# Branch projections released token tile by token tile, with the linear attention's norm ahead of the branch products

## What is computed

```python
z = rms_norm(x, ln_mix) @ w_in
o_nsa = nsa_attention(...)            # branch 0
o_gla = gated_linear_attention(...)   # branch 1: rms_norm(o, norm_g) * silu(r) at its end
o_mem = memory_attention(...)         # branch 2
gates = sigmoid(merge + b_merge)
merged = (gates[:, :, 0] * (o_nsa @ w_branch[0])
          + gates[:, :, 1] * (o_gla @ w_branch[1])
          + gates[:, :, 2] * (o_mem @ w_branch[2]))
x = x + merged @ w_out
```

## Time and profile before

| | us |
|---|---|
| median of 3 runs | 1996.36 |
| lowest, highest | 1995.1, 1997.03 |
| the profiled execution | 1997.19 |
| its span in the trace | 1995.5 |
| PE busy | 1960.1 (98%) |
| POOL busy | 1593.1 (80%) |
| ACT busy | 1045.1 (52%) |
| DVE busy | 750.8 (38%) |

### The profile page before, as it was taken

How to read it: one execution, slowest core, us unless ns; L and a number is a source line. 1 busy time by engine, 2 the same in 40 slices (tenths; PEclk the granted TensorE clock), 3 DMA queues, 4 the chain that set the end, 5 groups by cost and what they waited for, 6 DMA issues and landing times.

```text
span 1995.5 us, 26511 instructions
## 1 busy us (share of the span) xinstructions
PE 1960.1 (98%) x9698; PEld 1583.3 (79%) x9698; DVE 750.8 (38%) x1652; ACT 1045.1 (52%) x1748; POOL 1593.1 (80%) x1160
## 2 busy tenths in 40 slices
PE   9999999999999999999999999899999999999999
PEld 7888777888888877788887777788888777778887
DVE  4534444000300444400055688521115478742111
ACT  6445666444644566644475444654446554555443
POOL 7888876988788887698879577888888867788886
PEclk9999999999999999999999999999999999999999
DMA  6655434555665543456564333456547333345553
GB/s 234 232 206 179 159 117 157 186 186 188 211 218 190 174 157 125 166 196 240 190 253 148 117 116 127 138 182 222 208 169 274 127 127 117 119 136 195 184 186 131
DMA packets 98204, 348.63 MB, mean 175 GB/s; under 512 B 13436, under 2 KB 14108, under 8 KB 97820
## 3 DMA queue, kind: packets, MB, share of 16 engines
q1 hardware_dynamic: 97372, 345.80, 50.2%
q10 hardware_dynamic: 704, 1.14, 0.2%
HBM read 345.85 MB, written 1.05 MB: 174 GB/s over the span
## 4 chain that ended last, share of the span: by engine, by line
PE 93%; DVE 3%; POOL 2%; issue 1%; ACT 1%; DMA 0%; SPq 0%; DVEq 0%; ACTq 0%; POOLq 0%
PE psum L569 28%; PE psum L571 27%; PE psum L570 27%; PE psum L707 2%; POOL lo L542 2%; PE psum L750 1%; PE psum L637 1%; PE psum L760 1%; PE psum L982 1%; PE psum L773 1%; PE psum L740 1%; DVE big L2142 0%; PE psum L1136 0%; PE psum L837 0%; PE psum L796 0%
## 5 line engine op out<-in xcount | busy, mean ns | idle before, releaser
L542 POOL TENSOR_TENSOR lo<-raw,hi 128x256 fp32r<-128x256 f32 (+1 forms) x1156 | 1592.9, 1401 | 388.2 <-ACT hi L1270 359.6
L1270 ACT ACTIVATE hi<-raw 128x1024 fp32r<-128x1024 f32 x616 | 647.8, 1059 | 507.3 <-PE psum L571 482.8
L569 PE MATMUL psum<-hi,h_hi 128*128 128x512 f32 x1632 | 654.0, 401 | 2.3 <-POOL lo L542 2.1
L571 PE MATMUL psum<-hi,h_lo 128*128 128x512 f32 x1632 | 640.6, 393 | 0.0
L570 PE MATMUL psum<-lo,h_hi 128*128 128x512 f32 x1632 | 639.4, 392 | 0.0
L569 PEld LDWEIGHTS psum<-hi,h_hi 128*128 128x128 f32 x1632 | 308.7, 189 | 72.9 <-POOL lo L542 6.0
L571 PEld LDWEIGHTS psum<-hi,h_lo 128*128 128x128 f32 x1632 | 308.0, 189 | 66.2
L570 PEld LDWEIGHTS psum<-lo,h_hi 128*128 128x128 f32 x1632 | 308.6, 189 | 60.3
L1811 DVE SCALAR_TENSOR_TENSOR big<-psum,small,big 128x256 f32<-128x256 f32 (+1 forms) x120 | 61.1, 551 | 749.5 <-ACT big L1363 749.5
L569 PE MATMUL psum<-hi,y_hi 128*128 128x512 f32 x832 | 334.3, 402 | 8.4 <-DVE big L2262 4.9
L571 PE MATMUL psum<-hi,y_lo 128*128 128x512 f32 x832 | 325.5, 391 | 0.0
(11 more groups left out here) (265 smaller groups left out, 1396.1 us busy)
## 6 DMA issues: line engine op xcount, KB each, us to landing
raw<-in_stream SPq DMA_DIRECT2D x616, 512.0 KB, 3.3
big<-in_w SPq DMA_DIRECT2D x14, 512.0 KB, 6.9
big<-in_post SPq DMA_DIRECT2D x6, 512.0 KB, 5.3
special<-in_b_merge SPq DMA_DIRECT2D x2, 1536.0 KB, 8.1
memkv<-in_mem SPq DMA_DIRECT2D x2, 1024.0 KB, 5.7
big<-in_band SPq DMA_DIRECT2D x2, 768.0 KB, 4.8
x<-in_x SPq DMA_DIRECT2D x2, 512.0 KB, 5.0
special<-in_special SPq DMA_DIRECT2D x2, 512.0 KB, 4.4
```

Of the source, the lines that this page charges most:

```text
L542: t = pool.tensor_tensor(M.lo[:, slot, w], M.raw[:, slot, w], f32(M.hi[:, slot_hi, w]), ALU.subtract)
L569: pe.matmul(out, lhs_hi, rhs_hi, start=start, stop=False)
L571: return pe.matmul(out, lhs_lo, rhs_hi, start=False, stop=stop)
L1270: act.activation(M.hi[:, slot_hi, :], M.raw[:, slot, :], ACT.Copy).then_inc(sem["hi"], 1)
```

## The change

Three things. The tiles' banks are now given as a pair, and for branches 2 and 0 tile 0 goes to banks 2, 3 and tile 1 to 0, 1. PE waits before each tile for that tile's banks alone, and tells DVE by a new semaphore `rows` when tile 0 of a branch's last piece is done. And the steps of the linear attention's norm stand earlier: `gla` 3 to 5 behind pieces 61 and 62 (before: 62 to 64), 6 and 7 behind 64 and 65 (before: 65 and 66), with the table load of Ln and Exp right behind the last gate.

```diff
-ROWS2 = {2: 0, 0: 0, 1: 4}
+ROWS2 = {2: (2, 0), 0: (2, 0), 1: (4, 6)}
...
-        ("rows", 2): ([nu[17], gu[1][4]], [nu[18]], [gla[3]], [gla[4]]),
-        ("rows", 0): ([gla[5]], [gla[6]], [gla[7]], none),
+        ("rows", 2): ([nu[17], gu[1][4]], [nu[18], gla[3]], [gla[4], gla[5]], none),
+        ("rows", 0): ([gla[6]], [gla[7]], none, none),
...
-            t = product(psum[:, bank + 2 * m + i, :], a_hi[:, kt, m * P:m * P + P], a_lo[:, kt, m * P:m * P + P],
+            t = product(psum[:, banks[m] + i, :], a_hi[:, kt, m * P:m * P + P], a_lo[:, kt, m * P:m * P + P],
...
-    def rows(c, kt, a_hi, a_lo, bank, start, stop=False, second=None):
+    def rows(c, kt, a_hi, a_lo, banks, start, stop=False, second=lambda: None):
 
         pe.wait_ge(sem["lo"], c + 1)
         for m in range(MT):
-            if m and second:
-                pe.wait_ge(sem[second[0]], second[1])
-            t = rows_tile(c, m, kt, a_hi, a_lo, bank, start, stop)
+            if m:
+                second()
+            t = rows_tile(c, m, kt, a_hi, a_lo, banks, start, stop)
+            if stop and m == 0:
+                t.then_inc(sem["rows"], 1)
         t.then_inc(sem["used"], 1)
...
+                second = lambda: None
                 if b == 2 and i == 0:
-                    evicted(len(names) + 1)
                     evicted(len(names))
+                    second = lambda: evicted(len(names) + 1)
                 if b == 0 and i == 0:
-                    pe.wait_ge(sem["branch"], 4 * layer + 2)
+                    pe.wait_ge(sem["branch"], 4 * layer + 1)
+                    second = lambda: pe.wait_ge(sem["branch"], 4 * layer + 2)
...
                     act.activation(w, w, ACT.Sigmoid).then_inc(sem["sigmoid"], 1)
-            elif what == "branch":
-                if step[1:] == (2, 0):
+                if b == 1:
                     exp_and_ln()
...
-                dve.wait_ge(sem["used"], piece["rows", b, 3] + 1)
+                if m:
+                    dve.wait_ge(sem["used"], piece["rows", b, 3] + 1)
+                else:
+                    dve.wait_ge(sem["rows"], nxt("rows"))
```

More of the change, by code:

```diff
@@ L214 @@
 SEMAPHORES = (
-    "hi", "lo", "used", "quarter",
+    "hi", "lo", "used", "rows", "quarter",
     "x_in0", "x_in1", "ident", "const", "rot", "pre1", "pre2", "par", "mem_in", "masks", "angles", "stored", "w1_0", "w1_1",
@@ L585, in strip_piece, with rows_tile @@
         t.then_inc(sem["used"], 1)
-    def rows_tile(c, m, kt, a_hi, a_lo, bank, start, stop):
+    def rows_tile(c, m, kt, a_hi, a_lo, banks, start, stop):
         slot, slot_hi = c % RING, c % RING_HI
@@ L591, in rows_tile, with half_rows @@
             w = slice(i * 512, i * 512 + 512)
-            t = product(psum[:, bank + 2 * m + i, :], a_hi[:, kt, m * P:m * P + P], a_lo[:, kt, m * P:m * P + P],
+            t = product(psum[:, banks[m] + i, :], a_hi[:, kt, m * P:m * P + P], a_lo[:, kt, m * P:m * P + P],
                         hi[:, slot_hi, w], lo[:, slot, w], start, stop)
         return t
-    def rows(c, kt, a_hi, a_lo, bank, start, stop=False, second=None):
+    def rows(c, kt, a_hi, a_lo, banks, start, stop=False, second=lambda: None):
         pe.wait_ge(sem["lo"], c + 1)
         for m in range(MT):
-            if m and second:
-                pe.wait_ge(sem[second[0]], second[1])
-            t = rows_tile(c, m, kt, a_hi, a_lo, bank, start, stop)
+            if m:
[3 more added lines that the diff above has]
+                t.then_inc(sem["rows"], 1)
         t.then_inc(sem["used"], 1)
-    def half_rows(c, m, kt, a_hi, a_lo, bank, stop):
+    def half_rows(c, m, kt, a_hi, a_lo, banks, stop):
         if m == 0:
             pe.wait_ge(sem["lo"], c + 1)
-        t = rows_tile(c, m, kt, a_hi, a_lo, bank, False, stop)
+        t = rows_tile(c, m, kt, a_hi, a_lo, banks, False, stop)
         if m:
@@ L613, in half_rows, with last_rows @@
             t.then_inc(sem["f"], 1)
-    def last_rows(c, kts, a_hi, a_lo, bank, turn, ylo={}):
+    def last_rows(c, kts, a_hi, a_lo, banks, turn, ylo={}):
         for m in range(MT):
@@ L622, in last_rows @@
                     pe.wait_ge(sem["ylo"], ylo[i])
-                half_rows(c + i, m, kt, a_hi, a_lo, bank, i == len(kts) - 1)
+                half_rows(c + i, m, kt, a_hi, a_lo, banks, i == len(kts) - 1)
     def turned_tile(src, m, pairs, banks, ready, until):
@@ L713, in down @@
             for i in range(kts):
-                rows(c + i, (s - n0) % 2 * kts + i, y_hi, y_lo, 4, s == n0 and i == 0)
+                rows(c + i, (s - n0) % 2 * kts + i, y_hi, y_lo, (4, 6), s == n0 and i == 0)
         c += 4
@@ L730, in feed_forward @@
         order = [(strips - s) % 2 * kts + i for s in ((2, 1) if gated else (1,)) for i in range(kts)]
-        last_rows(c, order, y_hi, y_lo, 4, turn_next, {kts: n0 + strips} if gated else {})
+        last_rows(c, order, y_hi, y_lo, (4, 6), turn_next, {kts: n0 + strips} if gated else {})
         return c + 4
@@ L903, in mix1 @@
                 pe.wait_ge(sem["y1lo"], 7 * layer + Y1_EVENT[kt])
-                rows(c0 + 24 + i, kt, y_hi, y_lo, 0, i == 0, second=("z5", layer + 1) if i == 0 else None)
+                rows(c0 + 24 + i, kt, y_hi, y_lo, (0, 2), i == 0, second=lambda: pe.wait_ge(sem["z5"], layer + 1))
             elif what == "half":
@@ L908, in mix1 @@
                 pe.wait_ge(sem["y1lo"], 7 * layer + Y1_EVENT[kt])
-                half_rows(c0 + 24 + KD - 4 + i, m, kt, y_hi, y_lo, 0, i == 3)
+                half_rows(c0 + 24 + KD - 4 + i, m, kt, y_hi, y_lo, (0, 2), i == 3)
             elif what == "turn":
@@ L1202, in mix2 @@
                 pe.wait_ge(sem["y2lo"], 10 * layer + Y2_EVENT[kt])
-                rows(piece[step], kt, y_hi, y_lo, ROWS2[b], i == 0, i == 3)
+                rows(piece[step], kt, y_hi, y_lo, ROWS2[b], i == 0, i == 3, second)
             elif what == "last_branch":
@@ L1211, in mix2 @@
                 enter(V.merged, (0, 1, 2, 3), "merged", 4 * layer, c,
-                      lambda cc, m, j: rows_tile(cc, m, j, h_hi, h_lo, 4, j == 0, False), lambda j: j // 2)
+                      lambda cc, m, j: rows_tile(cc, m, j, h_hi, h_lo, (4, 6), j == 0, False), lambda j: j // 2)
                 pe.wait_ge(sem["xlo"], 8 * n["feats"])
-                last_rows(c + 4, range(4, KD), h_hi, h_lo, 4, turn_next)
+                last_rows(c + 4, range(4, KD), h_hi, h_lo, (4, 6), turn_next)
                 c += KD
@@ L2260, in branch @@
             dve.wait_ge(sem["sigmoid"], 6 * layer + 2 * (2, 0, 1).index(b) + m + 1)
-            bank = ROWS2[b] + 2 * m
+            bank = ROWS2[b][m]
             t = dve.tensor_tensor(g, g, flat(psum[:, bank:bank + 2, :]), ALU.mult)
```

## The result

| | before | changed |
|---|---|---|
| median, us | 1996.36 (7 runs) | 2000.45 (7 runs) |
| lowest, highest, us | 1992.92, 1998.26 | 1999.59, 2003.58 |
| span of the profiled execution, us | 1995.5 | 2001.0 |
| its mean granted clock | 0.994 | 0.992 |

The ratio is 1.0026, 95% interval 1.0017 to 1.0035: about 5 us more (3.4 to 7.0), and the medians differ by 4.1 us.

A forecast was written before the change was run, and what follows sets the result against it. PE was taken as the bound (93% of the chain that ended last). +2.49 us in the first layer and +1.97 in the second, +4.46 on the median 1996.36, gave 2000.8 us; range 1997.5 to 2004.0.

The forecast's parts named there:

- Part 1: PE's wait ahead of piece 60: tile 0 runs before the SiLU ends, so piece 63 ends 1.37 us earlier.
- Part 2: PE's wait ahead of piece 64: the norm delays DVE's product, so PE resumes at 1269.63, 1.97 us later than before.
- Part 3: Clock behind the stop at piece 64: falls in both layers, 1.27 us more in the first, nothing new in the second.
- longer low clock: Rival: clock low for longer behind that stop and DVE loses the race with POOL; 2004.5 us, chance 0.16.
- Part 4: What comes behind, to w_out's fourth piece: PE resumes 5.21 us after w_out's start; +2.49 us first layer, +1.97 second.
- The clock spares the kernel: Rival: the clock stays at 1.00 behind the stop at piece 64 in both layers; 1998.3 us, chance 0.18.
- The release by tiles does nothing: Rival: tile 0 of piece 60 is still held, piece 63 ends at 1265.21; time as forecast, within its 0.55.
- Not slower: Rival: the norm is ready in time and both stops go, POOL giving most back; 1994.4 us, chance 0.11.

The follow-up runs named there:

- e1: The changed kernel with the norm's steps and table load put back where they stood, release by tiles kept: 1992.22 us, ratio 0.9983 to the kernel before.
- e3: The changed kernel with the norm's guess and second multiply behind branch 2's products, its transposes behind pieces 65 and 66: 1994.34 us, ratio 0.9992 to before.
- e2: The kernel before with only the norm's steps and the table load moved forward, no release by tiles: 2007.1 us, ratio 1.0053.
- e5: The changed kernel with 20 matmuls nobody reads added on PE ahead of the wait before piece 64: 1998.51 us, ratio 1.0009 to before.
- e6: The changed kernel with squares and norm behind piece 67's rounding, both transposes behind piece 66, the second waiting for its own bank only: 1991.75 us, ratio 0.9976 to before.
- e9: e6 with the squares and the rest of the norm behind the rounding of piece 68 too: 1992.43 us, ratio 0.9975 to before.
- e7: e3 with POOL subtracting pieces 66 to 75 of the second mixer in one instruction each instead of four: 2004.86 us, ratio 1.0043 to before.

## Why the prediction was right

The forecast was 2000.8 us and the measured median 2000.45, with the ratio at 1.0026. Point by point:

**Part 1** held: 0.38 us of stop inside piece 60 where 0.3 was said, and the end of piece 63 moved as worked out.

**Part 2** held to 0.13 us. Exp ends at 1267.39 - 0.96 = 1266.43 (said: 1266.40), the four steps take 0.2 us each, the multiply is the short one (1.23), and PE resumes at 1269.76 (said: 1269.63). That the multiply came ahead of POOL was close, by 0.10 us where 0.3 was worked out. e1 and e3 show that it is the norm's place ahead of the products that makes the stop, since it goes in e1, and shrinks to 0.63 us in e3, when that is put back; e2 shows that the move does harm by itself.

**Part 3**, the clock, was right in kind and too small in size. The sum took 1.27 us in each layer with a fall, the price of the one row at hand. Measured from piece 64 to `w_out`: 26.34 us in the first layer (1297.06 - 1270.72), against 24.54 before, and e5, without a fall, 1.93 us less at the fourth piece. So the term was 1.8 to 1.9 us in the first layer and not 1.27. The stretch of half clock had begun while PE still stood and reached 4.1 us into its work. In the second layer it reached 2.9 us, and there the term held: 25.78 us against 25.81 before, which had its own fall. The first layer's 1.8 to 1.9 us lie in the range that the prediction gave the term (up to 2.54), part of the way to the rival of the longer low clock.

**Part 4**, what is given back to POOL, held in kind. The resumption at the fourth piece came 5.60 us after the start of `w_out` in both layers (said: 5.21). POOL took no longer over piece 75: from its start on it to PE's resumption there are 3.76 us (1298.90 to 1302.66), and in the row of 5.21 there were 3.77 (1785.67 to 1789.44). What came later was ACT's rounding of the piece, 0.68 us behind the start of `w_out` instead of 0.28:

```profile
1296.62 0.66 PE L639 MATMUL psum<-consts,big 128*128 128x128 f32 x4 [0.42 <-DVE big L2275]
```

```profile
1297.74 2.03 ACT L1274 ACTIVATE hi<-raw 128x1024 fp32r<-128x1024 f32 x2
```

```profile
1785.67 6.07 POOL L542 TENSOR_TENSOR lo<-raw,hi 128x256 fp32r<-128x256 f32 x5 [0.35 <-ACT hi L1270]
```

```profile
1298.90 6.05 POOL L542 TENSOR_TENSOR lo<-raw,hi 128x256 fp32r<-128x256 f32 x5 [0.34 <-ACT hi L1274]
```

The first of the two POOL lines is of the kernel before, second layer; the others are of the changed kernel. ACT rounds behind its casts of the turned `merged`, and PE had stood 0.42 us for DVE's addition to `merged` in the middle of the turning, in both layers; in the row used there was no such stop.

The sum by terms, first layer: 3.54 (said 2.49: +0.13 wait, +0.53 clock and +0.39 here). Second layer: 2.47 (said 1.97: +0.14 wait, -0.03 clock and +0.39 here). The sum for the profiled execution was thus short by 1.5 us. It stood at 2002.66, 2.2 us above the median of its kernel, so that the median nevertheless is 0.35 us from the forecast owes something to luck: in its sum the errors add up to more than in its result.

**The rivals.** "The clock spares the kernel" fell, as it did not spare it in either layer of the profiled execution; some of the other runs may have been spared in part. Four of the seven stand at 1999.6 to 2000.5 us with a mean clock of 0.994 or 0.995, the median among them, and three at 2002.4 to 2003.6 with 0.992, the profiled one among them. None of the four has a trace, so how much of the clock term is in the median is open; e5, which keeps PE busy in that stop, comes out some 3 us lower by the ratios, so the timed runs seem to pay for the clock too, but the two intervals just touch. "Longer low clock" was met halfway in the first layer, without the lost race on DVE. "The release by tiles does nothing" fell with the 0.38 us inside piece 60: tile 0 had run, and piece 63 ended 1.37 us earlier. "Not slower" fell with the date of Exp. Its number for a kernel without the stops was 1994.4; e1 came to 1992.2 and e3 to 1994.3, so the idea behind it, that POOL gives most back, was sound.

**A version that beats both** is e6 (or e1 and e9, which aren't told apart from it): 0.24% below the kernel before, and by the two ratios 0.5% below the changed one. In the changed place itself the traces show 2.5 us for e6 and 5.3 for e9.

## What to carry to other kernels

When work is moved forward in an engine's fixed order, ask what it waits for, and then everything that now stands behind it waits for the same thing: here two products of 1.2 us, which PE needed, stood behind a norm that hung on ACT's Ln and Exp, at the end of 17 us of other work on ACT. A release by finer parts is worth its freed waits only up to the next bound, and that bound may be an engine that is not the busiest over the whole span (POOL 80%, PE 98%): the date at which ACT's roundings, 52% busy, let POOL begin set the time 30 us later. A stop of PE can cost more than its length, since PE may resume at half the clock (here 1.9 us more, by e5).

## What the runs showed of the hardware

Small DVE instructions beside POOL were dearer than I had allowed. The norm's four small steps took 0.17 to 0.18 us each with POOL idle (changed kernel), 0.56 to 0.67 beside POOL's quarters (e6), and three of them 2.1 to 2.3 beside POOL's whole pieces (e7), where each ended with the POOL instruction under way.

```profile
1266.66 0.56 DVE L1720 TENSOR_TENSOR small<-small 128x8 f32<-128x8 f32 x1
1267.26 0.66 DVE L1721 TENSOR_TENSOR small<-small 128x8 f32<-128x8 f32 x1
1267.95 0.67 DVE L1722 TENSOR_SCALAR small<-small 128x8 f32<-128x8 f32 x1
```

These are e6's. In the Trainium skill, "SBUF — State Buffer", section "Who interferes with whom", this is the rule that the second to issue blocks until the first is done. By that a short instruction can wait for a long one, and the trace agrees. The TENSOR_SCALAR on cells of 128x8 waited as the others did, 2.27 us beside POOL's whole pieces.

The granted clock also fell behind e6's stop of 1.98 us, in both layers and in both of its profiled executions, and behind the 1.25 us stop between the layers in the kernel before (not in the changed one). It had stayed at 1.00 behind the 2.45 us stop of the first layer before, and in both layers behind 2.02 us in e3 and behind 2.79 us in e1. The length of the stop alone doesn't decide it in these traces.
